# A second numerator bank pair, two score banks and kept scores in an mLSTM recurrence, with four changes of instruction order

## The reference

```python
def modulation(cond, w, b):
    m = jax.nn.silu(cond) @ w + b
    return m.reshape(cond.shape[0], 1, N_MOD, D_MODEL)

def swiglu(h, w13, w2):
    a, g = jnp.split(h @ w13, 2, axis=-1)
    return (jax.nn.silu(g) * a) @ w2

def mlstm_scan(q, k, v, log_i, log_f, C0, n0, m0):       # 4 heads, chunks of 128 tokens
    def step(carry, inp):
        C, n, m = carry
        qb, kb, vb, ib, fb = inp
        bcum = jnp.cumsum(fb, axis=-1)
        a = bcum + m[..., None]
        Dm = jnp.where(tril, bcum[..., :, None] - bcum[..., None, :] + ib[..., None, :], -jnp.inf)
        m_t = jnp.maximum(a, jnp.max(Dm, axis=-1))
        w_inter = jnp.exp(a - m_t)
        Wd = jnp.exp(Dm - m_t[..., None])
        s = jnp.einsum('bhtd,bhsd->bhts', qb, kb) * Wd
        num = w_inter[..., None] * jnp.einsum('bhtd,bhde->bhte', qb, C) + jnp.einsum('bhts,bhse->bhte', s, vb)
        den = w_inter * jnp.einsum('bhtd,bhd->bht', qb, n) + jnp.sum(s, axis=-1)
        h = num / jnp.maximum(jnp.abs(den), jnp.exp(-m_t))[..., None]
        w_last = Wd[..., -1, :]
        wi_last = w_inter[..., -1]
        C_new = wi_last[..., None, None] * C + jnp.einsum('bhs,bhsd,bhse->bhde', w_last, kb, vb)
        n_new = wi_last[..., None] * n + jnp.einsum('bhs,bhsd->bhd', w_last, kb)
        return (C_new, n_new, m_t[..., -1]), h
    (C, n, m), hs = lax.scan(step, (C0, n0, m0), (chunks(q), chunks(k), chunks(v), chunks(log_i), chunks(log_f)))

def ab_mixer_latent(h, k_ctx, v_ctx, C0, n0, m0, w_in, w_out, rpb, gate_b, hnorm):
    qa, ka, va, qm, km, vm, om, gates = jnp.split(h @ w_in, AB_SPLITS, axis=-1)
    a_out = na_latent(qa, ka, va, k_ctx, v_ctx, rpb)
    m_out, _, _, _ = mlstm_mixer(qm, km, vm, om, gates, gate_b, hnorm, C0, n0, m0)   # scan forward and backward
    return jnp.concatenate([a_out, m_out], axis=-1) @ w_out
```

## Time and profile before

| | us |
|---|---|
| median of 3 runs (lowest, highest) | 2494.33 (2493.68, 2495.67) |
| the profiled execution | 2489.8 |
| its span | 2488.0 |
| TensorE busy in it | 2420.6 |
| DVE, ACT, POOL busy | 1769.2, 909.0, 347.4 |

### The profile page before, as it was taken

The page is one execution under the profiler, slowest core; times in us unless marked ns, Lnnn a source line. Parts: engine busy times, 40 slices in busy tenths (PEclk is TensorE's granted clock), DMA queues, the critical chain, the costliest instruction groups (busy, mean ns, idle before and its releaser), DMA issues. The chain is left out here.

```text
span 2488.0 us, 38914 instructions
## 1 busy us (share of the span) xinstructions
PE 2420.6 (97%) x14856; PEld 2227.7 (90%) x14856; DVE 1769.2 (71%) x2701; ACT 909.0 (37%) x1745; POOL 347.4 (14%) x373
## 2 busy tenths in 40 slices
PE   6999999999999899999999999999999999999998
PEld 5998999789989789979988998899899979989997
DVE  4887588858454769887855988786567559856863
ACT  4211121343343554423435442343421154423432
POOL 0000000110121421202202220121200021201211
PEclk9999999999999999999999999999999999999999
DMA  6544455435222323263342326333244323243332
GB/s 241 161 143 134 129 152 163 134 111 148 72 57 73 93 98 94 64 218 100 86 154 81 88 68 212 102 86 124 80 144 136 104 83 103 69 149 98 86 125 95
DMA packets 359638, 289.76 MB, mean 116 GB/s; under 512 B 38918, under 2 KB 317334, under 8 KB 358454
## 3 DMA queue, kind: packets, MB, share of 16 engines
q1 hardware_dynamic: 359478, 287.59, 38.2%
HBM read 275.32 MB, written 12.18 MB: 116 GB/s over the span
## 5 line engine op out<-in xcount | busy, mean ns | idle before, releaser
L2031 DVE TENSOR_TENSOR w_lo<-w_raw,w_hi 128x512 fp32r<-128x512 f32 (+2 forms) x287 | 259.4, 905 | 295.9 <-ACT w_hi L1445 292.9
L1445 ACT ACTIVATE w_hi<-w_raw 128x512 fp32r<-128x512 f32 (+2 forms) x287 | 228.9, 800 | 603.4 <-PE psum L1035 213.3
L960 PE MATMUL psum<-w_hi,act_hi 128*128 128x512 f32 x800 | 319.4, 399 | 8.9 <-DVE w_lo L2031 8.7
L962 PE MATMUL psum<-w_hi,act_lo 128*128 128x512 f32 x800 | 317.2, 396 | 0.0
L961 PE MATMUL psum<-w_lo,act_hi 128*128 128x512 f32 x800 | 317.0, 396 | 0.0
L1035 PE MATMUL psum<-hT_hi,w_hi 128*128 128x320 f32 x1216 | 278.3, 310 | 0.6 <-DVE w_lo L2031 0.5
L1035 PE MATMUL psum<-hT_hi,w_lo 128*128 128x320 f32 x1216 | 277.1, 309 | 0.0
L1035 PE MATMUL psum<-hT_lo,w_hi 128*128 128x320 f32 x1216 | 276.9, 309 | 0.0
L1079 PE MATMUL psum<-hT_hi,w_hi 128*128 128x320 f32 x684 | 211.6, 309 | 1.6 <-DVE z_quarters L2314 1.6
L1080 PE MATMUL psum<-hT_lo,w_hi 128*128 128x320 f32 x684 | 211.4, 309 | 0.0
L1081 PE MATMUL psum<-hT_hi,w_lo 128*128 128x320 f32 x684 | 211.3, 309 | 0.0
(11 more groups left out here) (299 smaller groups left out, 5309.4 us busy)
## 6 DMA issues: line engine op xcount, KB each, us to landing
w_raw<-in_ffn_w_dram SPq DMA_DIRECT2D x116, 512.0 KB, 4.4
w_raw<-in_ffn_w_dram SPq DMA_DIRECT2D x148, 256.0 KB, 2.9
w_raw_next<-in_ffn_w_dram SPq DMA_DIRECT2D x60, 512.0 KB, 5.4
ada_raw<-in_ada_w_dram SPq DMA_DIRECT2D x56, 512.0 KB, 3.6
ada_tile_ffn<-in_ada_w_dram SPq DMA_DIRECT2D x40, 512.0 KB, 4.7
w_raw<-in_ab_w_in_dram SPq DMA_DIRECT2D x28, 512.0 KB, 4.2
w_raw<-in_sc_w_in_dram SPq DMA_DIRECT2D x24, 512.0 KB, 4.1
ada_first<-in_ada_w_dram SPq DMA_DIRECT2D x4, 2048.0 KB, 18.9
```

What stands on the lines that cost most here:

```text
L960: mm(out, a_hi, b_hi, start=first, stop=False)
L962: return mm(out, a_lo, b_hi, start=False, stop=final)
L1445: A(dst, src, ACT.Copy).then_inc(w_hi_ok, 1)
L2031: V.tensor_tensor(d_, a, b.bitcast(F32), ALU.subtract).then_inc(w_lo_ok, 1)
```

## The change

It has five parts. (1) In the recurrence the numerators alternate between PSUM banks 4, 5 and 2, 3 (`NUM_BANK`), so `back(q)` waits for `h_sum` of q-2 instead of q-1. Scores use banks 0 and 1 alone, and ACT copies three score tiles to SBUF (`scores_kept`, a new instruction each, `sc_kept`), from which steps 5, 6 and 7 read. TensorE runs `products(q+2)` behind `back(q)` instead of ahead of it. ACT takes `w_inter` of steps 0 and 1 first and then `w_inter` of q+2 within step q, ahead of `head_squares` and `w_hi`. POOL takes `q_scaled` of step 1 ahead of two masked decays. (2) The opening's modulation matmuls are spread between the transposes. (3) ACT makes `w_hi` of unit 0 ahead of the copies of the modulation rows. (4) In the six seven-product half-phases, ACT and DVE split out unit 1 together with unit 0, ahead of the last gated product. (5) In the mixing of layer 0 the first three `ada_tile_ab` loads move from unit 2 to units 4 and 5, two modulation steps move one unit earlier, and the context's keys and values and `m_prev` are loaded at unit 6 instead of 2.

```diff
@@ -88,3 +88,3 @@
-STEPS = {"ffn": [1 + j for j in range(16)], "ab": [2, 2, 3, 3, 4, 4, 5, 5, 7, 8, 9, 9, 10, 10, 11, 11], "sc": [2 + j for j in range(16)]}
+STEPS = {"ffn": [1 + j for j in range(16)], "ab": [2, 2, 3, 3, 4, 4, 5, 5, 7, 7, 8, 9, 10, 10, 11, 11], "sc": [2 + j for j in range(16)]}
@@ -92,3 +92,4 @@
-FIRST_LOAD, NEXT_LOAD = 2, {"ffn": 3, "ab": 2, "sc": 2}
+FIRST_LOAD = {"ffn": (2, 2, 2), "ab": (4, 4, 5), "sc": (2, 2, 2)}
+NEXT_LOAD = {"ffn": 3, "ab": 2, "sc": 2}
@@ -853,6 +856,2 @@
-dma(ktok[:], cache_k[0, 0].rearrange("h p d -> p h d")).then_inc(ctx_loaded, 16)
-dma(vctx[:], cache_v[0, 0].rearrange("h p d -> p h d")).then_inc(ctx_loaded, 16)
-dma(mprev[:, 0, 0:1], state_m[0, 0, 0].rearrange("(h a) -> h a", a=1), **slow).then_inc(m0_loaded, 16)
-dma(mprev[:, 1, CT - 1:CT], state_m[0, 0, 1].rearrange("(h a) -> h a", a=1), **slow).then_inc(m0_loaded, 16)
@@ -863,2 +862,7 @@
+if u == 6:
+    dma(ktok[:], cache_k[0, 0].rearrange("h p d -> p h d")).then_inc(ctx_loaded, 16)
+    dma(vctx[:], cache_v[0, 0].rearrange("h p d -> p h d")).then_inc(ctx_loaded, 16)
+    dma(mprev[:, 0, 0:1], state_m[0, 0, 0].rearrange("(h a) -> h a", a=1), **slow).then_inc(m0_loaded, 16)
+    dma(mprev[:, 1, CT - 1:CT], state_m[0, 0, 1].rearrange("(h a) -> h a", a=1), **slow).then_inc(m0_loaded, 16)
@@ -924,2 +928,11 @@
+def first_modulation(h):
+    pe.wait_ge(csil_ok, 1)
+    pe.wait_ge(ada_landed[h], 16)
+    for k in (2 * h, 2 * h + 1):
+        for i in range(PRO):
+            last = mm(PS[32 * i:32 * i + 2, i, :], csil[:, :, k], ada0[:, k, i * MODW:(i + 1) * MODW], start=(k == 0), stop=(k == KD - 1))
+    if h == KD // 2 - 1:
+        last.then_inc(mod_mm, 1)
+
@@ -932,9 +945,5 @@
-pe.wait_ge(csil_ok, 1)
-for k in range(KD):
-    if k % 2 == 0:
-        pe.wait_ge(ada_landed[k // 2], 16)
-    for i in range(PRO):
-        last = mm(PS[32 * i:32 * i + 2, i, :], csil[:, :, k], ada0[:, k, i * MODW:(i + 1) * MODW], start=(k == 0), stop=(k == KD - 1))
-last.then_inc(mod_mm, 1)
+    if t in (1, 3, 4):
+        first_modulation((1, 3, 4).index(t))
+first_modulation(KD // 2 - 1)
@@ -1133,5 +1142,6 @@
-    pe.wait_ge(ml_st, 8)
+    pe.wait_ge(ml_st, 3)
+    pe.wait_ge(sc_kept, 3)
 elif t < 2:
-    pe.wait_ge(ml_h, len(ML_STEPS))
+    pe.wait_ge(ml_h, len(ML_STEPS) - 1)
@@ -1334,4 +1344,5 @@
-if q == 2:
-    pe.wait_ge(in_evac[1], ph["iv_end"][1])
+if q in (2, 3):
+    pe.wait_ge(ml_st, q - 1)
+    pe.wait_ge(sc_kept, q - 1)
@@ -1348,4 +1359,6 @@
-if q:
-    pe.wait_ge(ml_h, q)
+if q >= 2:
+    pe.wait_ge(ml_h, q - 1)
+elif q == 1:
+    pe.wait_ge(in_evac[1], ph["iv_end"][1])
@@ -1357,3 +1370,3 @@
-o_ = PS[:, 4 + h // 2, (h % 2) * 256:(h % 2) * 256 + MLD + 1]
+o_ = PS[:, NUM_BANK[q % 2] + h // 2, (h % 2) * 256:(h % 2) * 256 + MLD + 1]
@@ -1374,5 +1387,5 @@
+back(q)
 if q + 2 in SCORE_STEPS:
     products(q + 2)
-back(q)
@@ -1500,2 +1513,3 @@
+split(plan[0][0]["nin"])
@@ -1503,3 +1517,2 @@
-split(plan[0][0]["nin"])
@@ -1547,3 +1560,3 @@
-for u in range(AB_SPLIT if ph.get("ab") else 1, len(units)):
+for u in range(AB_SPLIT if ph.get("ab") else 2 if seven(ph) else 1, len(units)):
@@ -1650,3 +1663,4 @@
-split(ph["nout"], shape="out", prod=slot_done(ph, 0))
+for u in range(2):
+    split(ph["nout"] + u, shape="out", u=u, prod=slot_done(ph, u))
@@ -1818,3 +1832,4 @@
-for q, (dr, cc) in enumerate(ML_STEPS):
+def inter(q):
+    dr, cc = ML_STEPS[q]
@@ -1822,2 +1837,4 @@
+else:
+    act.wait_ge(m_spread[q], 16)
@@ -1825,4 +1842,18 @@
+
+def keep_scores(i):
+    act.wait_ge(ml_st, i + 1)
+    A(Sk[i][:], PS[:, SCORE_BANK[i], :].rearrange("p (h t) -> p h t", h=MLH), ACT.Copy).then_inc(sc_kept, 1)
+
+inter(0)
+inter(1)
+keep_scores(0)
+keep_scores(1)
+for q, (dr, cc) in enumerate(ML_STEPS):
     if q + 2 < len(ML_STEPS):
         decay(q + 2)
+    if q == 1:
+        keep_scores(2)
+    if q + 2 < len(ML_STEPS):
+        inter(q + 2)
@@ -1950,9 +1981,13 @@
+def scaled_queries(q):
+    cc = ML_STEPS[q][1]
+    pool.wait_ge(ml_wi, q + 1)
+    if q >= 2:
+        pool.wait_ge(ml_num, q - 1)
+    pool.tensor_tensor(qs[:, q % 2], FT[:, 8:12, cc * P:(cc + 1) * P], wi[:, q % 2], ALU.mult).then_inc(ml_qs, 1)
+
 for q, (dr, cc) in enumerate(ML_STEPS):
     edge = P - 1 if dr == 0 else 0
-    if cc < CT:
-        pool.wait_ge(ml_wi, q + 1)
-        if q >= 2:
-            pool.wait_ge(ml_num, q - 1)
-        pool.tensor_tensor(qs[:, q % 2], FT[:, 8:12, cc * P:(cc + 1) * P], wi[:, q % 2], ALU.mult).then_inc(ml_qs, 1)
+    if cc < CT and q != 1:
+        scaled_queries(q)
@@ -1967,2 +2002,3 @@
+scaled_queries(1)
@@ -2397,3 +2434,4 @@
-split(ph["nout"], shape="out")
+for u in range(2):
+    split(ph["nout"] + u, shape="out", u=u)
@@ -2623,3 +2661,8 @@
-V.tensor_tensor(STs[:, q % 2], PS[:, SCORE_BANK[q], :].rearrange("p (h t) -> p h t", h=MLH), Wx[q % 4][:], ALU.mult).then_inc(ml_st, 1)
+if q in SCORE_KEPT:
+    dve.wait_ge(sc_kept, SCORE_KEPT[q] + 1)
+    src = Sk[SCORE_KEPT[q]][:]
+else:
+    src = PS[:, SCORE_BANK[q], :].rearrange("p (h t) -> p h t", h=MLH)
+V.tensor_tensor(STs[:, q % 2], src, Wx[q % 4][:], ALU.mult).then_inc(ml_st, 1)
@@ -2629,3 +2672,3 @@
-num = pair(4).rearrange("p a (b c) -> p (a b) c", b=2)
+num = pair(NUM_BANK[q % 2]).rearrange("p a (b c) -> p (a b) c", b=2)
@@ -2708,3 +2751,5 @@
-SCORE_BANK = [0, 1, 2, 3, 3, 2, 1, 0, 3, 3]
+SCORE_BANK = {0: 0, 1: 1, 2: 0, 3: 1, 4: 1, 8: 1, 9: 1}
+SCORE_KEPT = {5: 2, 6: 1, 7: 0}
+NUM_BANK = (4, 2)
```

More of the change, by code:

```diff
@@ L342, in build @@
             [where["silu_g"], where["u_tmp"], a3] + [hh + i * 2048 for i in range(5)] + [hl + i * 2048 for i in range(2)])]
+        Sk = [at(f"scores_kept{i}", [P, MLH, P], hl + 4096 + i * 2048) for i in range(3)]
         hssq = at("h_ssq", [P, NT * MLH], hl + half + 8192 + 480)
@@ L414, in build @@
         ones_ok, st_out = sem("ones_ok"), sem("st_out")
+        sc_kept = sem("sc_kept")
         h_ssq_ok, h_r_ok, h_n_ok, hT2_done, hT2_evac = (sem(n) for n in (
@@ L678, in load_mods @@
                 for j in range(8 * n):
-                    if (FIRST_LOAD if j < 3 else STEPS[kind][j - 3] + NEXT_LOAD[kind]) != u:
+                    if (FIRST_LOAD[kind][j] if j < 3 else STEPS[kind][j - 3] + NEXT_LOAD[kind]) != u:
                         continue
@@ L823, in _ @@
                             dma(raw[:, n % 2], sc_w_in[0].rearrange("(p k) n -> p k n", k=KD)[:, :, c0:c0 + P]).then_inc(w_loaded[n % 2], 16)
-                            if u == FIRST_LOAD:
+                            if u == FIRST_LOAD["sc"][0]:
                                 sp.wait_ge(hT_ready, HM(s, NT))
@@ L2214, in out_phase @@
                 for u in range(AB_SPLIT if ph.get("ab") else 1, len(units)):
-                    split(ph["nout"] + u, shape="out", u=u)
+                    if u > 1 or not seven(ph):
+                        split(ph["nout"] + u, shape="out", u=u)
                     if final and u == (4 if K == HF else AB_SPLIT):
```

## The result

The changed kernel is slower by a little: median 2497.53 us (2493.23 to 2501.92, 22 runs) against 2493.89 (2487.49 to 2497.44, 22 runs) before, ratio 1.0015, 95% interval 1.0009 to 1.0021. That is +3.6 us where -3.8 was forecast, within 0.2%, but above the range's upper end of 2497.0 and of the other sign. The profiled execution took 2497.7 us with a span of 2495.9. The two profiled executions are 7.9 apart, more than the medians, which are 3.6 apart: that of before was 4 us faster than its own median, so their difference is read by place and the size is taken from medians.

The account below looks back on a forecast made before the run. TensorE, busy 97% of the span, was taken as the bound, so only its waits could be won. Recurrence +3.6, opening -1.8, mixing -3.2, out unit 1 -2.4 gave -3.8: 2494.33 to 2490.5 us, range 2482 to 2497 (8 in 10).

Parts of the forecast that it names:

- Recurrence: Part 1: early steps gain 3, then step 7's queue chain on ACT and POOL makes a net loss of 3.6 us.
- N(1): Recurrence, numerators of step 1 on TensorE: forecast to start at 808.8, at full clock, against 811.17 before.
- N(7): Recurrence, numerators of step 7: forecast to start at 838.9 instead of 836.05, after TensorE idles 5.9 us.
- a step's least: Recurrence, middle steps: no step can go under about 3.8 us while POOL has this work.
- Opening: Start of the kernel: spread modulation matmuls and earlier w_hi of unit 0 start the columns earlier, gain 1.8 us.
- 16 matmuls, 2.0: Opening: only the last quarter of the 64 modulation matmuls is left after the last load, taking 2.0 us.
- Mixing: Mixing's projection: the 2.9 us wait at unit 3 and a 0.8 wait go, less 0.45 at unit 5: gain 3.2.
- By hand 557.6 against a need of 557.2, loss 0.45: Mixing, unit 5: w_lo ready at 557.6 behind loads and four DVE steps, needed at 557.2, costing 0.45 us.
- Out unit 1: Out-projections: six waits of 1.06 to 1.07 at unit 1 go, partly moving to unit 2: gain 2.4 us.
- The wait moves there whole: Out-projections: where unit 2's w_lo was already late behind a load, unit 1's wait moves to unit 2 whole, 1.06.
- Slower: Rival, 0.12: TensorE's clock stays at 1.2 GHz from N(7) or N(6) until out unit 1 ends; total +9.0, 2503.3.
- not at 562: Mixing rival, 0.10: loads pile up, w_lo of unit 5 comes at 562; +1.3 instead of -3.2, total +0.7, 2495.0.

Follow-up runs that it names:

- ab_only: Kernel before with only part 5, the mixing's loads and modulation steps: median 2493.76 us, ratio 1.0002.
- out_only: Kernel before with only part 4, the earlier split of out unit 1 in six half-phases: median 2496.70 us, ratio 1.0008.
- out_load: out_only plus out unit 2's load issued ahead of the gate and norm loads in three second half-phases: 2485.89 us, ratio 0.9966 to the kernel before.
- rec_pool: rec_only with POOL's head root one step later, behind the next q_scaled and v_weighted: 2494.74 us, ratio 1.0003 to the kernel before.
- rec_only: Kernel before with only part 1, the recurrence (bank pairs, kept scores, order of ACT and POOL): median 2497.66 us, ratio 1.0010.
- rec_banks: rec_only's banks, kept scores and TensorE order, but ACT's and POOL's order of the kernel before: 2493.55 us, ratio 0.9996 to the kernel before.
- rec_fill: rec_only plus 48 useless matmuls behind the scores of step 8, ahead of N(7): 2503.40 us, ratio 1.0032 to the kernel before.
- rec_all: rec_pool with ACT's w_hi and squares ahead of w_inter of q+2, and DVE's head scaling one step later: 2488.48 us, ratio 0.9978 to the kernel before.

## Why the prediction was wrong

- **Recurrence, right in its mechanism, too small.** The loss of 3.6 came at 4.8 within its stretch. N(0) came 0.7 earlier than before, so I count from it. N(1) was forecast 3.7 after it and came 3.65 after; N(7) was forecast 33.8 after it and came 34.9; from N(7) to the end 10.3 were forecast and 10.4 came. So the missing 1.2 lies ahead of N(7), and 0.9 of it in one step: N(4) to N(5), 821.5 to 825.0 in the forecast, which is 3.5 and less than the 3.8 that the same text gives as a step's least, took 4.41. The step that failed is the price of the kept scores. I priced their three copies (nothing, in ACT's idle stretches) and not their reads, and the first read took 1.75 where scores from PSUM take 0.69, which is 1.06 more and ends just as N(5) starts.
- **Opening, 1.8 forecast, 0.8 measured (1.0 alone).** The step that failed is "16 matmuls, 2.0": spread out, they have a gap of 3.18 ahead of the last quarter, the granted clock is then 0.56, and they take 3.32.
- **Mixing, 3.2 forecast, about 0.5 by medians.** The 2.9 at unit 3 came. "By hand 557.6 against a need of 557.2, loss 0.45" failed: `w_lo` of unit 5 was ready at 559.6, a wait of 1.99, since the third tile let DVE's steps begin only at 553.4, and behind it the clock was low (0.56; in ab_only, after a wait of 1.52, it was full).
- **Out unit 1, -2.4 forecast, +2.4 by the median of out_only (-0.5 to +4.5): the largest miss.** That four of the six waits move to unit 2 and two vanish came true. "The wait moves there whole" took the landing of unit 2's load as fixed, and this step failed: in the three second half-phases it landed 0.5 to 1.1 later after its issue, the waits there came to 2.57, 2.21 and 2.09, and behind the first two the granted clock was 0.61 and 0.58. By waits alone the gain was gone (8.9 against 8.7); the clock, which the sum left out, turns it to a loss by the median. out_load shows that this load is what mattered: with it early, load and split together are worth 8.8.
- I priced the clock in one place only, behind the largest gap. It was low behind grown waits in four more places: the opening, unit 5 and two of the out units.
- By the medians of the parts alone the misses are -0.2, +1.1, +2.7 and +4.8 (recurrence, opening, mixing, out units), 8.4 in sum, against 7.4 for the whole. None of the rivals with a price is what happened: the low clock of "Slower" came, but was at 0.90 again in the 2.4 us behind N(7), and `w_lo` of unit 5 came at 559.6, not at 562.
- The profiled execution of before was one of its faster ones; I noted the 4.5 and gave it no part in the range.

## What to carry to other kernels

When an edit takes away a wait, look up what is late next and also which transfers the edit sets free at that moment, since they may compete with the one that is late. A second bank removes one edge of a circle; the gain shows only when each in-order queue has its instructions in the order in which the others need them, and here two moved instructions (rec_pool against rec_only, 2.4 us) were worth more than the banks with the kept scores that they need (rec_banks against before, 0.2 us longer). When a tile moves from PSUM to SBUF, price its reads as well as the copy. A wait that grows can cost more than its length, and one that is removed can give back more.

## What the runs showed of the hardware

TensorE's granted clock fell behind the same wait in some executions and not in others. Of 13 profiles that have the mixing's wait at unit 3 (2.6 to 3.4 us), seven show 1.2 GHz in the microseconds behind it; of the four kernels without the wait none at that place. The length of the wait doesn't decide: the longest, 3.39 in rec_only, was followed by full clock, the shortest, 2.59 in rec_fill, by 0.58 over 2 us. Nor does the code: eight of the 13 kernels are the same up to the recurrence, and three of these show it. Two of the eight, rec_only and rec_all, at the matmuls behind the wait:

```profile
545.30:549.30 4.00, 3.92 (x27) 3.92 (x28) 3.90 (x6) 0.15 (x1) 0.00 (x0) 1.00 0.38 100
```

```profile
543.70:547.70 4.00, 4.00 (x17) 4.00 (x16) 3.90 (x6) 0.00 (x0) 0.00 (x0) 0.50 0.47 131
```

27 matmul records start in the first and 17 in the second. One such stretch cost 1.5 to 2.7 us. With several such places in a kernel this can be a good part of the spread of 10 us and more between its executions: of the 110 executions of the kernel before that ran beside the experiments, the 16 with a mean granted clock of 0.992 have a median of 2497.6, the ten with 0.996 one of 2490.6. That it is the spread's only source was not tested.

A DVE product of two tiles in SBUF was slow beside POOL's work. The scores of step 5 took 1.75 to 1.77 in all ten kernels that keep scores, each time while POOL ran `q_scaled` or a masked decay, which took 1.71 to 1.80 instead of 1.27. The `w_lo` products, which also take two tiles from SBUF, took 0.68 to 1.86 in the recurrence. With POOL idle the read of the scores took 0.68, and scores from PSUM took 0.68 or 0.69 in every kernel, whether POOL ran or not.
